# Weighted one-hot columns: from one tensor operand and two scalars to two tensor operands and one scalar

## The reference

```
s, i = lax.top_k(scores, 16)                 # two halves of 128 keys for each of 8 heads
top_s, sel = lax.top_k(s1[:, None] + s2[None, :], 16)
idx  = i1 * 128 + i2                         # 8 x 16 = 128 experts for each token
gate = softmax(top_s)
act  = gelu(einsum('td,ted->te', h, u[idx]))
out  = einsum('te,ted->td', gate * act, v[idx])
```

## Time and profile before

| | us |
|---|---|
| median of 3 runs | 4019.97 (4017.22 to 4025.73) |
| the profiled execution | 4015.35 |
| its span | 4013.6 |
| PE busy | 3871.0 |
| DVE busy | 3028.2 |
| ACT busy | 2268.4 |
| POOL busy | 1070.5 |

### The profile page before, as it was taken

One profiled execution on the slowest core, in us unless ns is written; L12 is line 12 of the kernel. 1 busy time (PEld: TensorE's weight loads), 2 busy tenths in 40 slices (PEclk: granted clock), 3 DMA queues, 4 the chain that ended last, 5 costly groups with the idle time before them and its releaser, 6 DMA issues.

```text
span 4013.6 us, 76989 instructions
## 1 busy us (share of the span) xinstructions
PE 3871.0 (96%) x27054; PEld 3418.3 (85%) x27054; DVE 3028.2 (75%) x5829; ACT 2268.4 (57%) x4081; POOL 1070.5 (27%) x666
## 2 busy tenths in 40 slices
PE   6999999999999999999998999999998999999999
PEld 6898888888889888888888988888887788888887
DVE  6768889777566888976766787987775678797555
ACT  4256577545534656854556566865454556685554
POOL 0104458000010345810000244741000034482000
PEclk9999999999999999999998999999998999999999
DMA  8345553878514555387853555458882255534554
GB/s 286 129 142 187 185 167 130 280 255 284 169 50 137 173 188 173 127 274 243 288 173 116 175 182 192 137 198 294 285 285 108 75 179 183 192 125 165 192 192 155
DMA packets 203691, 749.53 MB, mean 187 GB/s; under 512 B 22704, under 2 KB 23856, under 8 KB 202192
## 3 DMA queue, kind: packets, MB, share of 16 engines
q1 hardware_dynamic: 178416, 646.51, 48.2%
q0 software_dynamic: 25056, 100.15, 7.8%
HBM read 745.52 MB, written 1.05 MB: 186 GB/s over the span
## 4 chain that ended last, share of the span: by engine, by line
PE 83%; POOL 7%; ACT 4%; DVE 4%; issue 1%; DMA 1%; POOLq 0%; SPq 0%; ACTq 0%; DVEq 0%
PE ps L2162 16%; PE ps L2632 12%; PE ps L2639 12%; PE ps L2635 12%; PE ps L2170 9%; POOL t_lo L658 4%; PE ps L2134 4%; PE ps L2135 3%; PE ps L2141 3%; ACT t_hi L736 3%; PE ps L2311 2%; PE ps L2566 2%; PE ps L2567 2%; POOL oh L651 1%; PE ps L2575 1%; POOL t_lo L636 1%
## 5 line engine op out<-in xcount | busy, mean ns | idle before, releaser
L736 ACT CAST t_hi<-raw 128x1024 fp32r<-128x1024 f32 x1180 | 1241.6, 1053 | 965.8 <-PE ps L2639 689.5
L1245 DVE TENSOR_TENSOR t_lo<-raw,t_hi 128x1024 fp32r<-128x1024 f32 x880 | 1077.0, 1225 | 590.9 <-ACT t_hi L736 570.8
L2162 PE MATMUL ps<-h_both,t_hi 128*128 128x512 f32 x3040 | 762.2, 393 | 0.0
L2162 PEld LDWEIGHTS ps<-h_both,t_hi 128*128 128x128 f32 x3040 | 546.6, 189 | 97.7
L636 POOL TENSOR_TENSOR t_lo<-raw,t_hi 128x1024 fp32r<-128x1024 f32 x176 | 450.7, 2561 | 625.5 <-ACT t_hi L736 625.5
L2632 PE MATMUL ps<-t_hi,h_both 128*128 128x512 f32 x2048 | 548.0, 389 | 5.4 <-DVE h_both L2023 5.4
L2639 PE MATMUL ps<-t_lo,h_both 128*128 128x512 f32 x2048 | 547.4, 389 | 0.0
L2635 PE MATMUL ps<-t_hi,h_both 128*128 128x512 f32 x2048 | 547.3, 389 | 0.0
L2134 PE MATMUL ps<-h_both,t_hi 128*128 128x256 f32 x1792 | 470.6, 299 | 24.2 <-DVE h_both L1419 11.8
L2632 PEld LDWEIGHTS ps<-t_hi,h_both 128*128 128x128 f32 x2048 | 384.0, 188 | 85.3 <-issue 6.1
L2635 PEld LDWEIGHTS ps<-t_hi,h_both 128*128 128x128 f32 x2048 | 384.5, 188 | 79.9
(11 more groups left out here) (325 smaller groups left out, 5178.6 us busy)
## 6 DMA issues: line engine op xcount, KB each, us to landing
raw<-u_tiles SPq DMA_DIRECT2D x512, 512.0 KB, 3.5
raw<-v_tiles SPq DMA_DIRECT2D x512, 512.0 KB, 4.2
raw<-w_tiles SPq DMA_DIRECT2D x188, 512.0 KB, 3.5
oh<-w_tiles POOLq DMA_DIRECT2D x160, 512.0 KB, 4.8
arena<-w_tiles SPq DMA_DIRECT2D x16, 512.0 KB, 4.0
arena<-keys_t POOLq DMA_DIRECT2D x4, 1024.0 KB, 6.8
arena<-mla_w POOLq DMA_DIRECT2D x1, 4096.0 KB, 14.5
arena<-lora POOLq DMA_DIRECT2D x2, 1280.0 KB, 8.8
```

What stands on the lines that cost most here:

```text
L736: act.copy(t_hi[:, j % SPL, :], raw[:, j % RAW, :]).then_inc(hi_done, 1)
L1245: tts(t_lo[:, j % SPL, :], raw[:, j % RAW, :], t_hi[:, j % SPL, :].bitcast(F32), ALU.subtract).then_inc(lo_done, 1)
L2162: mm(ps[:, j % 2, :], hi[:, c, :], h_both[:, c, :, :].rearrange("p a t -> p (a t)"), start=(c == 0), stop=False)
```

## The change

The operation with one tensor and two per-partition scalars is replaced by one with two tensors and one per-partition scalar. The comparison with the scalar stays; the weight, a column of one element per partition, is read as a tensor of 128 x 128 whose elements repeat along the row. POOL's column and ACT's three are as before, and so are all waits and the order.

```
                     for q in range(ACT_FROM - 1):
                         t = 8 * m + q
-                        ts(hot_cols[m % 2][:, q, :], iota, sel[:, 1, t:t + 1], sel[:, 2, t:t + 1], ALU.is_equal, ALU.mult)
+                        stt(hot_cols[m % 2][:, q, :], iota, sel[:, 1, t:t + 1], sel[:, 2, t:t + 1].broadcast_to([P, P]),
+                            ALU.is_equal, ALU.mult)
```

## The result

The changed kernel takes 4035.23 us (median of 7 runs, 4032.3 to 4038.42) against 4019.97 (7 runs, 4014.0 to 4025.73): ratio 1.0038, interval 1.0026 to 1.0049, so 15 us slower.

What follows compares the result with a forecast made beforehand. Bound: the gate-stage loop in which POOL's subtraction and VectorE's columns and rows hold each other. 0.07 + 0.03 = 0.10 us per period, times 120, gives +12.0 us: 4027.4 from the profiled execution, 4032 on the median's scale; range 4024 to 4048.

Steps and rivals of the forecast that it cites:

- The loop: Gate stage: E, four L1975 in 0.77, L1965's reading, rest of L658, next E; 0.77 + 3.48 = 4.25 us.
- E: Gate stage: the end of one POOL subtraction L658, from which each period of 4.25 us is counted.
- The ring in the chain of waits: Gate stage: L658 waiting for ACT's copy (24.1 us), TensorE for L651 (7.4 us); the copy wait not taken as bound.
- The first column, 0.07: First L1975 of each period: half rate paid in the open, ending at E + 0.15, the second starting 0.07 later.
- The spacing of the others "as now": Later L1975 of each period: step from start to start stays 0.26 us, the unrounded difference some 3 ns.
- the half rate: Each L1975: the two-tensor form takes 66 ns more for 128 elements, against 57 less for the scalar.
- The meeting with L651, 0.03: Columns against POOL's small L651: second column reads first, third loses 0 to 0.03 us, taken as 0.03.
- The sum: Gate stage: 0.07 + 0.03 = 0.10 us per period, times 120, +12.0 us.
- POOL winning the tie: Rival: L651 reads before the second column in every period; L1965 0.22 later, 26 us, 4046; chance 0.20.
- The hidden first column: Rival: first column's reading hidden or spaced as now; 0 to +2 us, 4021; chance 0.13.
- the whole of L651: Rival: all of L651 excludes the two-tensor form; second column 0.57 later, +77 us, 4097; chance 0.04.
- The faster rival: Columns: repeated operand is no second stream, POOL doesn't hold the new form, TensorE binds; 28 us less, 3992; chance 0.08.

Runs made afterwards that it cites:

- the first run: Kernel before, with POOL's weighted column (L651) replaced by a constant fill that reads nothing: 4015.55 us, ratio 0.9987.
- the first column alone: Kernel before, with only the first of the four columns in the new form, the other three in the old: 4026.73 us, ratio 1.0018.
- the fills: Changed kernel, with POOL's weighted column replaced by two constant fills that only write: 4032.41 us, ratio 1.0027.

## Why the prediction was right

- *The loop, from E over the four columns to the rows and 3.48 on.* Right. The 3.48 is there after the change, and it survived 0.65 us less work on POOL. The ring in the chain of waits, which I had set aside, was refuted by the first run. The periods between ends came out at 4.383, at the top of the 4.33 to 4.38 that were to show the loop, and the rows at E + 0.90, the top of 0.84 to 0.90.
- *The first column, 0.07.* Right: it ends at E + 0.15 and the second starts at E + 0.07, and the first column alone gives 0.065. Halving its width takes the 0.07 back.
- *The spacing of the others "as now".* Mis-sized by a little: 0.262 to 0.263 instead of 0.256, three times 0.006, which the sum had at nothing. The direction was in the text (3 ns, for which it shows no working), the size was half. The two figures behind it were good: the saved scalar, put at 57 ns, is 60 where both forms read from PSUM (0.402 and 0.341 each), and the half rate, put at 66, is the 0.065 by which the first column ends later.
- *The meeting with L651, 0.03.* Right in place and nearly in size. The second column is hardly held (0.347, against 0.339 when POOL only writes), the third is (0.372), and its successor starts 0.03 to 0.04 late. The measured share is 0.035 to 0.038. L651 is 0.08 longer, which costs nothing that the period shows, as said: the rows' start accounts for all of it.
- *The sum.* 0.10 forecast, 0.122 measured, 12.0 and 14.7 us. The median rose by 15.3, and 4035.2 stands against 4032. The two spans, less the 5.2 from before the first changed instruction, differ by 14.3, so the passing on to the end in full is borne out.
- *Rivals.* POOL winning the tie did not happen: the second column would be 0.45 long or more. The hidden first column is refuted, and so is the whole of L651 (L1965 would start at E + 1.4). The faster rival was wrong on the repeated operand: the first column is held (0.78) until E + 0.15, so it counts as a stream. Its figure of 3992 was right for a kernel in which the columns really are not held: 3991.4 with one of their two inputs in PSUM.
- *The rule of the Trainium skill in "SBUF — State Buffer", section "Who interferes with whom".* The measurement decides as before: against L658 whoever comes second waits to the end, against L651 it does not. Its distinction between reads and writes, by which a two-input instruction does not meet a GpSimd instruction that only writes, is what the fills show for the new form, 0.26 from start to start throughout.

## What to carry to other kernels

The engines of this kernel do not meet only through semaphores, as its opening has it: VectorE and POOL also hold each other up inside instructions that use SBUF, with no semaphore between them. When two engines share a way into SBUF, an instruction that is held counts as busy, and the profile names no wait for it. Look for durations that vary with the start while the end stays fixed to something on the other engine. Before changing the form of an instruction, ask what it shares: in these runs a double-rate instruction was held by POOL even when POOL only wrote, one with two SBUF tensors only when POOL read, and one with a single SBUF tensor at the single rate was not held at all. Putting a small constant operand in PSUM took more out of this loop than any choice between the forms.

## What the runs showed of the hardware that I had not expected

- A fill by POOL of 630 elements (0.62 us) holds VectorE's double-rate instruction, while it leaves the two-tensor one alone.
- The order between POOL's subtraction and VectorE's rows does not follow their recorded starts: with a lead of 0.06 us (0.08 at most) POOL was still second in every period, with 0.23 it was first.
- Past that point the stage doesn't become a little slower but changes its pattern: periods of 3.2 to 7.1 us and a mean of 4.8 to 5.0, from two runs in which POOL had less or other work, and 3.8 to 5.6 with a mean of 4.89 from the one with the rows first. In all three the subtraction had got ahead of one of VectorE's instructions.
